# Expert-down units in 512-column halves, with VectorE adding the halves between the steps of the picking

## The reference, cut to what matters

```python
def peer(h, w_query, sub_keys1, sub_keys2, expert_down, expert_up):   # 8 heads, top 16, 128 x 128 experts
    q = (hf @ w_query).reshape(T, PEER_HEADS, 2, D_KEY // 2)
    s1 = jnp.einsum("thk,hnk->thn", q[:, :, 0], sub_keys1)
    s2 = jnp.einsum("thk,hnk->thn", q[:, :, 1], sub_keys2)
    v1, i1 = lax.top_k(s1, PEER_TOPK)
    v2, i2 = lax.top_k(s2, PEER_TOPK)
    cand = (v1[..., :, None] + v2[..., None, :]).reshape(T, PEER_HEADS, PEER_TOPK * PEER_TOPK)
    top_s, pos = lax.top_k(cand, PEER_TOPK)
    gates = jax.nn.softmax(top_s, axis=-1)
    ...
    act = jax.nn.gelu(jnp.einsum("td,thkd->thk", hb, expert_down[ib]), approximate=False)
    return jnp.einsum("thk,thkd->td", gb * act, expert_up[ib])
```

## Time and profile before

| | |
|---|---|
| median of 3 runs | 1388.49 us (1388.33 to 1392.33) |
| the profiled execution | 1388.77 us, its span 1387.0 us |
| PE matmul busy | 1360.9 us, 98% of the span |
| DVE busy | 1044.9 us, 75% |
| ACT busy | 883.8 us, 64% |
| POOL busy | 654.1 us, 47% |

### The profile page before, as it was taken

The page is one execution under the profiler, slowest core; times in us unless marked ns, Lnnn a source line. Parts: engine busy times, 40 slices in busy tenths (PEclk is TensorE's granted clock), DMA queues, the critical chain, the costliest instruction groups (busy, mean ns, idle before and its releaser), DMA issues.

```text
span 1387.0 us, 31930 instructions
## 1 busy us (share of the span) xinstructions
PE 1360.9 (98%) x9728; PEld 1261.0 (91%) x9728; DVE 1044.9 (75%) x2247; ACT 883.8 (64%) x1847; POOL 654.1 (47%) x503
## 2 busy tenths in 40 slices
PE   7999999999999999999999999999999999999998
PEld 4799999999999989889999999999998888888886
DVE  6778867888988496559999778888876666666665
ACT  5668765555546666438888687777765555555554
POOL 4896783000006868688898887777730000000000
PEclk9999999999999999999999999999999999999999
DMA  9766565889983633564555544444445665665552
GB/s 345 272 251 230 198 243 184 329 320 318 335 332 122 212 130 117 188 226 168 181 181 181 181 168 157 161 152 151 156 166 193 196 192 190 193 196 192 190 193 91
DMA packets 79796, 283.82 MB, mean 205 GB/s; under 512 B 8821, under 2 KB 8949, under 8 KB 79610
## 3 DMA queue, kind: packets, MB, share of 16 engines
q1 hardware_dynamic: 79738, 283.07, 58.6%
HBM read 281.99 MB, written 1.05 MB: 204 GB/s over the span
## 4 chain that ended last, share of the span: by engine, by line
PE 83%; POOL 6%; issue 5%; DVE 3%; ACT 2%; DMA 1%; PEld 0%; PEldq 0%; POOLq 0%; SPq 0%; DVEq 0%
PE psA L1833 19%; PE psA L1837 19%; PE psA L1836 19%; PE psD L1833 6%; POOL w_lo L563 6%; PE psD L1836 6%; PE psD L1837 5%; PE psA L1883 2%; PE psD L2312 1%; PE psD L2313 1%; PE psA L1886 1%; PE psD L2269 1%; DMA xT<-x 1%; DVE arena L1539 1%; PE psA L1929 0%
## 5 line engine op out<-in xcount | busy, mean ns | idle before, releaser
L628 ACT CAST w_hi<-raw 128x512 fp32r<-128x512 f32 x864 | 529.5, 620 | 426.7 <-PE psA L1833 282.4
L563 POOL TENSOR_TENSOR w_lo<-raw,w_hi 128x512 fp32r<-128x512 f32 x476 | 633.3, 1351 | 351.7 <-ACT w_hi L628 341.1
L1833 PE MATMUL psA<-h_both,w_hi 128*128 128x256 f32 x1456 | 420.2, 289 | 0.6 <-POOL w_lo L563 0.5
L1836 PE MATMUL psA<-h_both,w_hi 128*128 128x256 f32 x1456 | 411.4, 283 | 0.0
L1837 PE MATMUL psA<-h_both,w_lo 128*128 128x256 f32 x1456 | 411.3, 282 | 0.0
L1098 DVE TENSOR_TENSOR w_lo<-raw,w_hi 128x512 fp32r<-128x512 f32 x388 | 266.3, 691 | 152.6 <-ACT w_hi L628 151.4
L1833 PEld LDWEIGHTS psA<-h_both,w_hi 128*128 128x128 f32 x1456 | 278.6, 191 | 4.3 <-issue 1.5
L1836 PEld LDWEIGHTS psA<-h_both,w_hi 128*128 128x128 f32 x1456 | 278.8, 191 | 0.1
L1837 PEld LDWEIGHTS psA<-h_both,w_lo 128*128 128x128 f32 x1456 | 278.5, 191 | 0.0
L1833 PE MATMUL psA<-w_hi,u_hi 128*128 128x512 f32 x512 | 199.4, 389 | 0.4 <-DVE u_lo L1161 0.4
L1837 PE MATMUL psA<-w_hi,u_lo 128*128 128x512 f32 x512 | 199.2, 389 | 0.0
(11 more groups left out here) (396 smaller groups left out, 2330.6 us busy)
## 6 DMA issues: line engine op xcount, KB each, us to landing
raw<-expert_down SPq DMA_DIRECT2D x128, 512.0 KB, 3.2
raw<-expert_up SPq DMA_DIRECT2D x128, 512.0 KB, 4.3
arena<-ada SPq DMA_DIRECT2D x96, 512.0 KB, 5.2
raw<-gateup SPq DMA_DIRECT2D x44, 512.0 KB, 5.2
raw<-feat SPq DMA_DIRECT2D x28, 512.0 KB, 3.7
raw<-win SPq DMA_DIRECT2D x24, 512.0 KB, 3.2
raw<-down SPq DMA_DIRECT2D x22, 512.0 KB, 6.0
raw<-wout SPq DMA_DIRECT2D x20, 512.0 KB, 3.7
```

What stands on the lines that cost most here:

```text
L563: nc.gpsimd.tensor_tensor(w_lo[:, s * HALF:(s + 1) * HALF], raw_half(n), w_hi[:, s * HALF:(s + 1) * HALF].bitcast(F32), ALU.subtract).then ...
L628: nc.scalar.copy(w_hi[:, n % SLOTS * HALF:(n % SLOTS + 1) * HALF], raw_half(n)).then_inc(hi_ready, 1)
L1833: first = mm(o, w[0], m[0], start=start, stop=False, skip_group_check=True)
L1836: mm(o, w[0], m[1], start=False, stop=False, skip_group_check=True)
```

## The change

Four things. TensorE runs units 0 to 61 as `joint_unit`. VectorE adds their halves (`add_halves`) at fixed places between the steps of the picking, into `U`, and these adds drain the banks; ScalarE's `activate` waits for the add and does the Gelu in place in `U`. To make room, the picking reads the scores where they are and writes values and indices where they are needed, without copies, and several small operands lie in PSUM (`v_ps`, `lead_ps`, `bits_ps`, `gates_ps`, `inverse_ps`); the layout of `eq` is turned, so that its steps write with a stride and its reduction reads in order. And at the start `add_nothing` adds ones times zeros to two banks, twice four matmuls of 128 columns.

```diff
-        eq = part(arena, 28672, TOPK, NT * QH, TOPK)
+        eq = part(arena, 28672, NT * QH, TOPK, TOPK)
...
+            def activate(dst, joint=True):
                 split(1)
-                A.free(nc.scalar.activation(dst, A.bank()[:, 0:T], ACT.Gelu))
+                if joint:
+                    A.count.n += 1
+                    act.wait_ge(a_drained, A.count.value())
+                    nc.scalar.activation(dst, dst, ACT.Gelu).then_inc(sem("early_acts"), 1)
+                else:
+                    A.free(nc.scalar.activation(dst, A.bank()[:, 0:T], ACT.Gelu))
...
+            def add_halves(n=1):
+                for _ in range(n):
+                    at = A_AT["experts"] + added.n
+                    added.n += 1
+                    dve.wait_ge(a_ready, at + 1)
+                    b = psA[:, at % BANKS, :]
+                    V.tensor_reduce(U[:, added.n - 1, :], b.rearrange("p (z t) -> p t z", z=2), AX.X,
+                                    ALU.add).then_inc(a_drained, 1)
...
-            with repeat(dve, QH, {own.count: NT * 20}) as h:
-                step(lambda t: V.tensor_copy(work[:, t, :, :], flat[:, bass.ds(h * 2 + t * 2 * QH, 2), :]))
+            for h in range(QH):
                 for z in range(2):
+                    top16(lambda t: v16[:, t, z, :], lambda t: top_i[:, h + t * QH, z, :],
+                          lambda t: scores[:, t, 2 * h + z, :], lambda t: work2[:, t, :])
+                    if z == 0:
+                        step(lambda t: V.tensor_copy(v_ps[:, t, :], v16[:, t, 0, :]))
+                    add_halves()
...
                 for i in range(TOPK):
-                    last = V.scalar_tensor_tensor(out=eq[:, i, :, :], in0=pick_ps, scalar=float(i),
+                    if i % 4 == 0:
+                        add_halves()
+                    last = V.scalar_tensor_tensor(out=eq[:, :, :, i], in0=pick_ps, scalar=float(i),
                                                   in1=idx[:, :, z, i:i + 1].broadcast_to([P, NT * QH, TOPK]),
                                                   op0=ALU.is_equal, op1=ALU.mult)
                 own(last)
-                own(V.tensor_reduce(picked[:, z, :], eq.rearrange("p i a k -> p (a k) i"), AX.X, ALU.add))
+                add_halves(2)
+                own(V.tensor_reduce(picked[:, z, :], eq.rearrange("p a k i -> p (a k) i"), AX.X, ALU.add))
+                add_halves(2)
...
+            add_halves(EARLY + 8 - added.n)
             dve.wait_ge(sem("gate_exp"), 2)
...
+            add_halves(P - LATE - 2 - added.n)
...
+            def add_nothing(bank, n):
+                for _ in range(n):
+                    mm(bank[:, 0:P], ones[:, :], mask_ts[:, 0:P], start=False, stop=False, skip_group_check=True)
+            add_nothing(banks[0][0], 4)
             pe.wait_ge(sem("x_sums"), 1)
...
+            add_nothing(banks[2][0], 4)
...
-            columns(A, P - LATE - 2, h_parts, ends=False)
+            with repeat(pe, (P - LATE - 2) // 4, {halves: 8, A.count: 4}):
+                for _ in range(4):
+                    joint_unit(A, h_both)
+            for _ in range((P - LATE - 2) % 4):
+                joint_unit(A, h_both)
```

More of the change, by code:

```diff
@@ L380, in two_mixers_program @@
         scores = part(arena, 28672, NT, 2 * QH, NK)
[L381 removed]
+        eq = part(arena, 28672, NT * QH, TOPK, TOPK)
         iota_k = rms[:, P:2 * P]
         top_v = part(late, 0, NT * QH, TOPK)
[L384 to L385 removed]
+        top_i = part(late, 256, NT * QH, 2, TOPK).bitcast(U32)
         idx = part(late, 768, NT * QH, 2, TOPK)
@@ L971, in _ @@
             act.wait_ge(sem("gate_args"), 1)
-            nc.scalar.activation(late[:, 0:T], picked[:, 2, :], ACT.Exp, scale=-1.0).then_inc(sem("gate_exp"), 1)
+            nc.scalar.activation(psD[:, 2, T:2 * T], psD[:, 2, 0:T], ACT.Exp, scale=-1.0).then_inc(sem("gate_exp"), 1)
             act.wait_ge(sem("gate_exp"), 1)
-            nc.scalar.activation(picked[:, 2, :], picked[:, 2, :], ACT.Exp).then_inc(sem("gate_exp"), 1)
+            nc.scalar.activation(psD[:, 2, 0:T], psD[:, 2, 0:T], ACT.Exp).then_inc(sem("gate_exp"), 1)
             hots = Count()
@@ L1633, in step, with top16 @@
                     dve.wait_ge(own.sem, own.count.value(1))
-                    dve.sem_inc(sem("top_steps"), 1)
                     fn(t).then_inc(own.sem, 1)
                     own.count.n += 1
-            def top16(vals, ids, src, spare):
+            added = Count()
+            def add_halves(n=1):
[6 more added lines that the diff above has]
+                                    ALU.add).then_inc(a_drained, 1)
+            def top16(vals, ids, src, spare, behind_second=True):
                 step(lambda t: V.max(vals(t)[:, 0:8], src(t)))
                 step(lambda t: V.max_index(ids(t)[:, 0:8], vals(t)[:, 0:8], src(t)))
+                if behind_second:
+                    add_halves()
                 step(lambda t: V.match_replace(spare(t), vals(t)[:, 0:8], src(t), LOWEST))
@@ L1656, in _ @@
                       lambda t: cand[:, t, :, :].rearrange("p a b -> p (a b)"), lambda t: cand2[:, t, :])
-                step(lambda t: V.tensor_copy(top_v[:, h + t * QH, :], v16[:, t, 0, :]))
-                step(lambda t: V.tensor_copy(pick_ab[:, h + t * QH, :], i16[:, t, 2, :]))
             dve.wait_ge(own.sem, own.count.value())
-            own(V.tensor_scalar(pick_u, pick_ab, 4, None, ALU.logical_shift_right))
+            own(V.tensor_copy(idx, top_i))
             for z in range(2):
-                if z == 1:
-                    own(V.tensor_scalar(pick_u, pick_ab, 15, None, ALU.bitwise_and))
-                own(V.tensor_copy(pick_ps, pick_u))
+                if z == 0:
+                    own(V.tensor_scalar(bits_ps, pick_ab, 4, None, ALU.logical_shift_right))
+                else:
+                    own(V.tensor_scalar(bits_ps, pick_ab, 15, None, ALU.bitwise_and))
+                own(V.tensor_copy(pick_ps, bits_ps))
```

37 lines of the change are left out of this document (18 added, 19 removed).

## The result

The changed kernel takes 1391.08 us (median of 13 runs, 1389.13 to 1393.9), the kernel before, timed beside it, 1388.49 (13 runs, 1387.8 to 1392.7). The ratio is 1.0017 with a 95% interval of 1.001 to 1.0025: slower by 0.17%, some 2.4 us, where a gain of 1.3 us was forecast. The profiled execution took 1390.93 us, its span 1389.1 us.

A forecast was written before the change was run, and what follows sets the result against it. TensorE, its matmuls busy for 98% of the span, was taken to bound the kernel. -4.9 + 0.7 + 1.1 + 0.2 + 2.6 - 1.0 = -1.3 us against 1388.77 gave 1387.5, median about 1387.2; range 1382 to 1392.

The forecast's parts named there:

- 3 x 0.25 = 0.7 us: Heads of ScalarE's four-unit turns: a long lag meets one about three times in 40, losing 0.7 us in all.
- the lag that is allowed, 1.7 us: Head of a turn: an add ending over 1.7 us after the next unit's start (its lag) reaches TensorE.
- 1.28 + 0.57 + 0.62 + 1.31 + 0.1: Head of a turn, add to TensorE: table load, Gelu and copy, cast, GpSimd's w_lo, signals.
- unit 40 heads a turn: 1.1 us lost: Add 40 stands behind a 256-wide pass's rest, a cast and two PSUM operations: lag 2.8 us, 1.1 us lost.
- Sum of the first term: 59 x (2.883 - 2.80) = 4.9 us: Expert-down stage on TensorE: 59 units shortened to 2.80 us by 512-column matmuls gain 4.9 us; ends 3.7 and 6.1.
- lag of 3.2 us: 0.2 us lost: Add of unit 46, behind VectorE's reduction of 4096 elements taken at 4.4 us: lag 3.2 us, 0.2 us lost.
- The rival's price of 2 x 3.3 us: Rival, chance 0.12: the two reductions stay at 7.7 us, 2 x 3.3 us on top, 1393.8 us in all.
- 2.6 us lost: Gates: no add between the 56th and the gates' last step, so TensorE loses 2.6 us at unit 59, 0.75 already at 58.
- I take 1.0: Start: added matmuls may raise TensorE's clock earlier, gaining between nothing and 2.2 us; 1.0 us taken.
- The spread writes: Rival, chance 0.1: steps writing 64 bytes apart take 0.54 us instead of 0.34, 1.1 us more, 1388.3 us.
- the first rival's best case: Rival, chance 0.2: VectorE's adds are never late; 1382.6 us, at the best -6.1 - 2.2, given as 1380.5 us.

The follow-up runs named there:

- e6_peel: Changed kernel with the first turn of ScalarE's loop written out ahead of it, so later turns hold no table load; ratio to the kernel before 0.9994.
- e9_no_adds: Changed kernel without VectorE's adds of the halves (product of w_hi with h_lo left out for 62 units); ratio to the kernel before 0.9974, stage 175.75 us.
- e4_eq_old: Changed kernel with `eq` laid out as before: steps write in order, reductions read 1 KB apart; ratio to the kernel before 1.0066, stage 186.90 us.
- e5_gate_adds: Changed kernel with the adds of units 56 and 57 moved earlier on VectorE at the gates; ratio to the kernel before 0.9996, stage 179.33 us.
- e12_split_reduce: Changed kernel with ScalarE's first turn written out, two gate adds moved, each big reduction cut in two with an add between; ratio to the kernel before 0.9968.
- e11_no_adds_peel: Changed kernel without VectorE's adds (w_hi with h_lo left out) and with ScalarE's first turn written out; ratio to the kernel before 0.9969, stage 175.33 us.

## Why the prediction was wrong

The mechanism was right: shorter work on TensorE, given back through late adds, casts and w_lo. The balance was off by 2.2 us in the stage (forecast -0.3, measured +1.95) and by 1.0 us at the start; the other 0.5 us between forecast and result are less than the intervals. The balance of the stage in the changed kernel's own trace is: pitch -4.3 us, heads of turns +2.25, unit 43 +1.1, unit 49 +0.36, gates +2.4, units 0 to 3 +0.2, which adds up to within 0.1 us.

**"3 x 0.25 = 0.7 us"** is the step that failed most. It measured 0.75 us ahead of units 18 and 19, 0.5 ahead of 23, 0.65 ahead of 38 and 39, and 0.1 in each of four others: 2.25 us. The place was right, the turn's head with its table loads, and e6_peel shows it. The lags were right too: 1.75 to 1.85 us for the long ones where I had 1.9. What was wrong is the lag that is allowed, 1.7 us. The way from an add to TensorE at unit 15, on VectorE, ScalarE and GpSimd (TensorE's matmul at 674.16 stands above):

```profile
669.30 0.67 DVE L1651 TENSOR_REDUCE arena<-psA 128x256 f32<-128x512 f32 x1
...
670.10 0.42 ACT L964 ACTIVATE arena<-arena  x1 [0.83 <-DVE arena L1651]
...
670.82 1.28 ACT L628 ACT_TABLE_LOAD   x1
672.12 1.14 ACT L628 CAST w_hi<-raw 128x512 fp32r<-128x512 f32 x2
...
672.81 2.54 POOL L563 TENSOR_TENSOR w_lo<-raw,w_hi 128x512 fp32r<-128x512 f32 x2 [1.26 <-ACT w_hi L628]
```

From 669.97 to 674.16 it is 4.19 us. The prediction's terms for this way, 1.28 + 0.57 + 0.62 + 1.31 + 0.1, make 3.88: Gelu and copy take 0.72 us with a table load behind them, not 0.57, and three hand-overs take 0.13, 0.07 and 0.08 us where 0.1 was counted. And two units last 5.54 us at the pitch here, not 5.60. So a lag of 1.75 us came 0.4 us late where the sum allowed it almost in full. The second matmul of each late unit then lost another 0.1 us, which the prediction did not have.

**"unit 40 heads a turn: 1.1 us lost"**: 1.1 us measured, ahead of unit 43, at a lag of 2.5 us, not 2.8. Part of the agreement is luck, since a lag that was shorter met a slack that was shorter too.

**"Sum of the first term: 59 x (2.883 - 2.80) = 4.9 us"**: 4.3 us measured over the 62 units, within the ends given. I averaged two pitches of the query stage, 2.78 and 2.82 us, as if they took turns. They are two levels, and one is kept over tens of units. The changed kernel's mean came to 2.81 because its stage had both. Where the upper level held throughout, as in e9_no_adds, 3.2 us were left of the gain, below my lower end of 3.7.

**"lag of 3.2 us: 0.2 us lost"** at the reduction: a lag of 3.1 and 0.36 us measured, and the reduction itself took 4.41 us for the 4.4 worked out. The rival's price of 2 x 3.3 us for reductions of 7.7 us met 6.0 us in e4_eq_old. Its mechanism held once: the first reduction gave 3.2 us, the second 1.95 us of waiting and some 1.6 us of a fallen clock, which the rival did not have.

**"2.6 us lost"** at the gates: 0.6 + 1.8 = 2.4 us measured, in the two places named. e5_gate_adds shows that the part at unit 59 hangs on the place of two adds, and e12_split_reduce that the part at unit 58 hangs on an add behind a whole reduction, not on the Exp alone.

**"I take 1.0"** for the start failed. It rested on the assumption that the added matmuls let the clock rise before or soon after the h matmuls begin. The profiled execution starts 0.6 us earlier, and keeps the slow pitch for 4.86 us as the kernel before did (4.85). The other traces and the runs show no gain.

**The spread writes** (chance 0.1) are dear, 0.61 us a step, more than the 0.54 worked out for that rival. The rule that the prediction quotes from the Trainium skill, SBUF — State Buffer, says that an access which crosses to a new line pays, and the trace agrees: 0.61 us a step for writes 64 bytes apart, 0.41 for writes in order. Their price for the time was 1.1 us, at the turn that begins at unit 44; no gap stands ahead of unit 47, for the lag was back to 0.65 us by unit 42. At unit 43 e4_eq_old shows that they cost nothing: there the add stands behind the cast and the two PSUM operations, ahead of the first step.

One slip changes nothing: the first rival's best case comes to 1388.77 - 0.3 - 6.1 - 2.2 = 1380.2 us, not 1380.5.

The remaining 0.9 us behind the stage (585.8 against 584.9 us) is within what executions differ: 584.2 to 586.1 us over these kernels.

## What to carry over

When work is moved onto an engine with slack, ask at each place how late its result may be, not how busy the engine is on average: these 62 adds cost 5.15 us in one order and 0.2 us in another (with the table loads out of ScalarE's loop), on an engine that idled 31 us of the stage. Read the whole way from the late result to the engine that waits in one place of a trace: a sum of single terms came out 0.3 us short here, and that made lags late that it had allowed. Look for what stands between the new wait and the next hand-over, above all a table load, which in this loop stood behind the wait; a loop whose last table is not its first pays two of them a turn. And read a pitch over a whole stretch before taking a mean: of two values seen once each, one may hold for the entire stage. The same goes for a wait or a clock in one execution: the one that was profiled first may be the odd one.

## What the runs showed of the hardware

- Pairs of a 512- and a 256-column matmul come every 0.347 us or every 0.353 us, for tens of units, at a granted clock of 1.00 in both. The level may change after a gap and differs between executions of the same instructions. Over 62 units that is 3.3 us. The three matmuls of 256 columns have one pitch only, 2.88 us a unit. The cause is open.
- An idle time may cost twice. In the changed kernel TensorE went from the 2.4 GHz level (0.23 us a matmul) back to 1.2 GHz (0.43 us) over 2.44 us of idling at the start, and in e11_no_adds_peel over 2.33 us. In e4_eq_old it did so over the idle 3.12 us ahead of 794.91, and not over the idle 3.30 us ahead of 769.33, so the length alone does not decide.
- VectorE: writes of fp32 64 bytes apart cost 606 ns per 256 elements against 414 in order; reads 1 KB apart 7.70 us per 4096 elements against 4.41 in order.
- The record of the granted clock can miss a slow stretch: from 20 to 22 us it reads 1.00 in twelve of the fourteen kernels and 0.50 in two, the changed kernel and e11_no_adds_peel, while the h matmuls come every 0.43 us there in all fourteen.
